# Gate/up pairs of a Strassen-Winograd feed-forward block: two kept products are added to each other by an accumulating SBUF transfer, and one low-part subtraction is issued later

## The reference, cut to what matters

```python
def swiglu(x, g, w_gu, w_down):
    gu = rmsnorm(x, g) @ w_gu
    return (jax.nn.silu(gu[..., :D_FF]) * gu[..., D_FF:]) @ w_down

# in trunk, for each layer i
x = x + swiglu(x, g_ffn[i], w_gu[i], w_down[i])
```

## Time and profile before

| | |
|---|---|
| median of three runs | 1248.07 us (1246.15 to 1248.12) |
| profiled execution, its own time | 1249.83 us |
| its span, first to last instruction | 1248.1 us |
| PE busy | 1216.1 us, 97% |
| DVE busy | 981.7 us, 79% |
| ACT busy | 655.7 us, 53% |
| POOL busy | 79.9 us, 6% |
| mean granted TensorE clock | 0.992 |

### The profile page before, as it was taken

How to read it: one execution, slowest core, us unless ns; L and a number is a source line. 1 busy time by engine, 2 the same in 40 slices (tenths; PEclk the granted TensorE clock), 3 DMA queues, 4 the chain that set the end, 5 groups by cost and what they waited for, 6 DMA issues and landing times. The chain is left out here.

```text
span 1248.1 us, 23025 instructions
## 1 busy us (share of the span) xinstructions
PE 1216.1 (97%) x8976; PEld 1170.6 (94%) x8976; DVE 981.7 (79%) x1600; ACT 655.7 (53%) x1178; POOL 79.9 (6%) x110
## 2 busy tenths in 40 slices
PE   6999999999999999999999999999999999999996
PEld 6997999999999999999989976799999999999996
DVE  4766558999999999975765476556999999999972
ACT  6656434454555555556754367533555555555542
POOL 1000000001001001102001100000001000100102
PEclk8998999999999999999999999999999999999998
DMA  7244122216425433525343210022225433532622
GB/s 223 81 132 128 35 85 85 68 51 147 111 71 125 116 94 94 139 85 155 133 129 122 88 65 2 1 85 85 68 60 132 119 90 95 126 102 82 157 64 85
DMA packets 196915, 122.13 MB, mean 98 GB/s; under 512 B 6091, under 2 KB 189035, under 8 KB 196808
## 3 DMA queue, kind: packets, MB, share of 16 engines
q1 hardware_dynamic: 185800, 101.24, 27.7%
q0 software_dynamic: 10816, 19.36, 6.8%
q10 hardware_dynamic: 192, 0.06, 0.0%
HBM read 106.67 MB, written 6.90 MB: 91 GB/s over the span
## 5 line engine op out<-in xcount | busy, mean ns | idle before, releaser
L1055 ACT ACTIVATE WH<-RAW 128x1024 fp32r<-128x1024 f32 (+2 forms) x149 | 144.2, 968 | 147.0 <-PE ACCP L1751 119.7
L1073 ACT ACTIVATE EH<-SB 128x1024 fp32r<-128x1024 f32 (+1 forms) x116 | 112.6, 971 | 166.7 <-DVE SB L1385 86.7
L1360 DVE TENSOR_TENSOR WL<-RAW,WH 128x1024 fp32r<-128x1024 f32 (+2 forms) x149 | 166.1, 1115 | 37.1 <-ACT WH L1055 35.9
L1391 DVE TENSOR_TENSOR EL<-SB,EH 128x1024 fp32r<-128x1024 f32 (+1 forms) x116 | 128.7, 1110 | 5.1 <-ACT EH L1073 2.8
L1751 PE MATMUL ACCP<-XH,WH 128*128 128x288 f32 x512 | 112.1, 301 | 3.7 <-DVE XL L1494 3.7
L1751 PE MATMUL ACCP<-XL,WH 128*128 128x288 f32 x512 | 110.3, 297 | 0.0
L1751 PE MATMUL ACCP<-XH,WL 128*128 128x288 f32 x512 | 110.3, 297 | 0.0
L1761 PE MATMUL MISC<-BH,EH 128*128 128x288 f32 x360 | 106.8, 297 | 1.6 <-DVE EL L1391 1.5
L1761 PE MATMUL ACCP<-BH,EH 128*128 128x288 f32 x360 | 106.8, 297 | 0.0
L1761 PE MATMUL MISC<-BL,EH 128*128 128x288 f32 x360 | 106.2, 295 | 0.0
L1761 PE MATMUL ACCP<-BL,EH 128*128 128x288 f32 x360 | 106.2, 295 | 0.0
(11 more groups left out here) (318 smaller groups left out, 3445.1 us busy)
## 6 DMA issues: line engine op xcount, KB each, us to landing
RAW<-in_w_gu SPq DMA_DIRECT2D x88, 512.0 KB, 3.9
RAW<-in_w_down SPq DMA_DIRECT2D x48, 384.0 KB, 4.2
RAW<-in_w_in SPq DMA_DIRECT2D x16, 512.0 KB, 4.4
RAW<-in_w_mem_kv SPq DMA_DIRECT2D x16, 512.0 KB, 3.6
RAW<-in_w_out SPq DMA_DIRECT2D x16, 512.0 KB, 4.1
X<-PC POOLq DMA_DIRECT2D x48, 144.0 KB, 2.9
RAW<-in_w_down SPq DMA_DIRECT2D x16, 256.0 KB, 2.9
RAW<-in_w_kv SPq DMA_DIRECT2D x8, 512.0 KB, 3.8
```

The source lines that it names most:

```text
L1055: a.activation(panel_in(WH, w % SPLIT_SLOTS, p), panel_in(RAW, p % RAW_SLOTS, p), ACT.Copy).then_inc(split_ready(w, True)[0], 1)
L1073: a.activation(EH[:, first:first + n, 0:nh], mixtures(s)[:, first:first + n, 0:nh], ACT.Copy).then_inc(block_hi, n)
L1360: v.tensor_tensor(panel_in(WL, w % SPLIT_SLOTS, p), panel_in(RAW, p % RAW_SLOTS, p), panel_in(WH, w % SPLIT_SLOTS, p), ALU.subtract).then_ ...
L1391: v.tensor_tensor(EL[:, first:first + n, 0:nh], mixtures(s)[:, first:first + n, 0:nh], EH[:, first:first + n, 0:nh], ALU.subtract).then_in ...
```

## The change

There are two parts.

1. In gate/up pairs `third_sum` is gone. Once all three copies are made, POOL issues a transfer that adds PC 1 to PC 2 in SBUF (semaphore `kept_summed`), and `second_sum` waits for that and adds U1 and the sum. The semaphore `up_right`, which `third_sum` raised, is replaced by `u_ready` where others waited for it.
2. `blocks_lo(k0)` is no longer issued after lead (3, 0), but in the first pair behind `hidden` of the last lead.

```diff
-                   (3, 0): [("lo", 6), ("blocks_lo", k0)], (3, 1): []}
+                   (3, 0): [("lo", 6)], (3, 1): []}
...
-            return (up_right, s.c + 1) if s.which == "gu" else (x22_done, 16 * (s.c + 1))
+            return (u_ready, 2 * s.i + 2) if s.which == "gu" else (x22_done, 16 * (s.c + 1))
...
+                elif s.kind == "pair" and s.which == "gu":
+                    gp.wait_ge(copied, 3 * s.i + 3)
+                    gp.dma_start(PC[:, s.i % 2, 2], PC[:, s.i % 2, 1], accum_op=ALU.add).then_inc(kept_summed, 16)
                 elif s.kind == "pair" and s.which == "down":
...
             def second_sum(s):
-                dve.wait_ge(copied, 3 * s.i + 3)
+                dve.wait_ge(kept_summed, 16 * (s.c + 1))
                 dve.wait_ge(u_ready, 2 * s.i + 1)
                 v.tensor_tensor(TU[:, HALF:T], U1[:], PC[:, s.i % 2, 2], ALU.add).then_inc(u_ready, 1)
-
-            def third_sum(s):
-
-                dve.wait_ge(u_ready, 2 * s.i + 2)
-                v.tensor_tensor(TU[:, HALF:T], TU[:, HALF:T], PC[:, s.i % 2, 1], ALU.add).then_inc(up_right, 1)
...
-                elif s.kind == "prepare_blocks_lo":
-                    blocks_lo(s.k)
...
                         take_lead(s.before)
                         split_lo(s.before.sn + 2)
                         hidden(s.before)
+                        blocks_lo(s.layer * HPAIRS * MIXED_PARTS)
...
                     if s.which == "gu":
                         second_sum(s)
-                        third_sum(s)
```

More of the change, by code:

```diff
@@ L726, in encoder_kernel @@
         block_done, copied = sem("block_done"), sem("copied")
-        u_ready, up_right, crossed = sem("u_ready"), sem("up_right"), sem("crossed")
+        u_ready, kept_summed, crossed = sem("u_ready"), sem("kept_summed"), sem("crossed")
         gate_right = sem("gate_right")
```

## The result

The changed kernel took 1254.2 us, median of 6 runs (1251.99 to 1257.67); the kernel before, on the same chip, 1248.28 us (6 runs, 1246.15 to 1249.89). The ratio is 1.0048, with a 95% interval of 1.0036 to 1.0059: slower by about 6 us, where 1247.2 us was forecast and the range ended at 1250.8. It is the sign of rival C, 2 us beyond that rival's own figure. The profiled execution took 1254.47 us, its span 1252.4 us.

The account below looks back on a forecast made before the run. PE, busy 97% of the span, was taken as the bound, with at most 7.6 us to gain from a faster DVE. Terms -0.3 - 1.2 + 0.6 = -0.9 us from 1248.07 gave 1247.2 us, range 1244.8 to 1250.8 us.

Parts of the forecast that it names:

- rival C: Last gate/up pair of each layer: its transfer is late and the kernel slower, +4.1 us, 1252.2 us; chance 0.11.
- Start of the layer, -0.3 us: Up to the first down pair: first EL wait shrinks, HBL wait grows; -0.13 us a layer, -0.3 us for both.
- small waits: PE at products 6 of pair 1 and 1 of pair 2: new waits, a few tenths each, none counting.
- Short waits, -1.2 us: Seven unlisted PE waits in gate/up pairs or the first down pair behind them: counted as gone, -1.2 us.
- DVE's relief: Whole kernel: DVE busy down by 16 us (36 x 0.46) with no gain in time to match.
- First gate/up pairs behind down pairs, nothing: Pair 17 and its like, six: sum there between 419.0 and 420.2, at most 0.2 us late; nothing lost.
- The last gate/up pair, +0.3 us a layer: Pairs 29 and 59: DVE waits for the transfer, PE loses 0.3 us a layer, +0.6 us; bounds 0 and 2.8.
- Pairs 28 and 58 ... nothing: 3.3 us between copy and second_sum, then 1 us in which DVE waits for PE: nothing lost.
- The end of the program: Around the span: 1.7 us taken over from the profiled execution before, with no term for the change.
- B: PE's waits in the pairs: DVE's relief reaches all of them, -7.6 us, 1240.5 us; chance 0.09 with half-way cases.
- D: Whole kernel: transfers slow weight loads as much as DVE gives, or short waits aren't DVE's; 1248.1 us, chance 0.10.
- The two rules of the Trainium skill: New transfer: some 2.3 us estimated, not used; GpSimd issue stalls during certain VectorE copies, two-input adds excepted.

Follow-up runs that it names:

- e1: Kernel before with all 36 third sums by transfer, low part of set k0 in its old place: 1249.74 us against 1248.04, ratio 1.0007.
- e2: Kernel before with only the low part of set k0 moved into the first pair, no transfers: 1251.43 us, ratio 1.0024.
- e7: Kernel before with transfers in the last three gate/up pairs of each layer alone (6 of 36), low part in its old place: 1251.54 us, ratio 1.0018.
- e8: Kernel before, no transfers, with ten extra second sums in the last gate/up pair of each layer: 1258.04 us, ratio 1.0074.
- e9: Kernel before with the transfer in the last gate/up pair of each layer alone (2 of 36): 1250.42 us, ratio 1.0006.
- e11: Kernel before with transfers only in the first gate/up pair behind each of the first two runs of down pairs (4 of 36): 1250.78 us, ratio 1.0010.
- e10: Kernel before, no transfers, with six extra second sums in the last gate/up pair of each layer: 1251.44 us, ratio 1.0026.
- e6: Changed kernel with the third w_down panel's load held until the layer's last transfer has landed: 1250.22 us, ratio 1.0010.
- first trace: Profiled execution of the changed kernel in its first measurement: 1254.47 us, span 1252.4 us.
- e3: Changed kernel with DVE's own third sum in the last gate/up pair of each layer, 34 transfers instead of 36: 1248.81 us, ratio 1.0003.
- e4: Kernel before with transfers only in chunks 4 to 6, 8 to 12 and 14 to 18 (26 of 36), low part in its old place: 1245.52 us, ratio 0.9971.
- Second trace: Profile from running the unmodified changed kernel once more: median 1253.53 us against 1249.29 for the kernel before, ratio 1.0034.

## Why the prediction was wrong, point by point

- *Start of the layer, -0.3 us*: -0.05 us a layer measured, -0.13 forecast. The chain was right in its steps: the first EL wait gone, the two "small waits" come (259 and 263 us). The HBL wait is as long as before, 1.0 us, and not the 2 us that stood among the signs: the small waits took the rest, for which the prediction had left room. The first down pair stands at 274.01 - 237.54 = 36.47 us from the start of the pairs against 36.02 before: +0.45 where +0.36 was worked out. e1 and e2 show the two halves, -1.48 and +1.43 us, against -1.47 and +1.34 in the terms: (3 x 0.49) and (2.16 less 0.82).
- *Short waits, -1.2 us*: not borne out, though the stretches look like it (-0.84 and -0.18 us over pairs 4 to 29 of the two layers). Most of it isn't the change's. The kernel before loses 0.76 us in pairs 9, 11 and 13 of layer 0 in its own trace; but e2, e7, e8, e9 and e11, in which DVE makes the third sum of those pairs itself, lose at most 0.09 us there, and only e10 has the loss again. In the traces of before and e10 ACT waited 2.0 us for a w_gu panel near 302 us, in the others at most 1.1 us; that this is the cause is argued, not shown. What the transfers do take away, in trace after trace, stands at the first down pair behind a row of gate/up pairs: 0.06 to 0.15 us each, some 0.2 us a layer, so 0.4 us in all. The term was read from one execution. The stretch of layer 0 varies by 2.0 us over the thirteen traces (259.8 to 261.8 us), with the transfer of pair 17 and with chance of this kind.
- *DVE's relief*: 16.8 us busy less, with no time gained to match. Right.
- *First gate/up pairs behind down pairs, nothing*: wrong in some executions. The sum was put at 419.0 to 420.2 us, from the typical and the slow row; it started at 420.29 in one trace (`cross` stood at 420.37 in the earlier trace rows: harmless), and 1.2 to 1.7 us later in three others, measured from the start of pair 4, where PE paid 1.4 to 1.9 us. The landing there was 6.0 to 7.5 us, more than the longest of the earlier trace rows.
- *The last gate/up pair, +0.3 us a layer*: this is the step that failed. The place and the queue behind it were right, and so, nearly, was the slack: 3.7 us by the prediction, 3.9 measured. The term, 0.6 us in all, was mis-sized three times over. First, it took a landing near the typical for a moment at which the DMA engines are always loaded. The trace of before had it, in a stretch cut to the transfer's own time, from the third copy's end on, and in the queue of SyncE:

```profile
537.60:540.90 3.30, 3.30 (x27) 3.30 (x27) 2.00 (x5) 0.41 (x1) 0.00 (x0) 1.00 0.76 224
```
```profile
536.08 1.47 SPq L915 DMA_DIRECT2D RAW<-in_w_down  x3
```

I had averaged over 7 us (0.38), and the half of it lies outside the burst. "Only the slowest of 48 landings is that slow" counted mostly quiet landings against a busy one; those of the last three pairs' transfers are 4.1 to 6.8 us. That it is the loads is shown by e6. By the slack of 3.9 us this alone cost 1.4 us in the first trace and 3.6 in the second. Second, it let the third copy end where it ended before. But ACT's copies stand behind FFNH, and DVE's earlier wait in pair 58 moved them 1.7 us. "Pairs 28 and 58 ... nothing" was true for PE directly (e3), and false for pair 59 behind; that is shown by e9 beside e7. It is so in layer 1 alone, and cost 1.7 us in the first trace and 1.0 in the second. Third, it priced PE's idle at its own length. Beyond it came some 1.5 us of half clock, in layer 1 of one trace of the change, and in both layers of e8. The term came to 0.48 + 4.05 = 4.5 us in one trace and 1.78 + 2.79 = 4.6 us in the other.
- *The end of the program*, put at nothing: the prediction took the 1.7 us around the span over from before, and no term for what 36 more transfers do there. Behind the last product stands a DRAIN of POOL, and the span ends 0.2 us behind it. Before, and with the change:

```profile
L536 POOLq DRAIN  x1: 4719/4719/4719, 1243.1 to 1243.1; - x1
```
```profile
L536 POOLq DRAIN  x1: 5495/5495/5495, 1246.7 to 1246.7; - x1
```

It rises with the number of new transfers, to within 0.1 us, whatever else the kernels do: 4.72 us with none (four traces) and with 4 (e11), 4.76 with 2, 4.80 with 6, 5.17 with 26, 5.41 with 34, and 5.50 us with 36 (four traces). Around the span the executions have 2.0 us with 36 transfers and 1.7 with none. Together that is 1.1 us of the loss. Why a DRAIN takes longer behind more transfers is open.
- *The rivals*: C had mechanism, place and sign. Its price of 2.8 us a layer came from one slow landing and left out the cascade and the clock; its chance of 0.11 was that of an accident, though the loads are there in every layer. By the rows above it deserved the larger chance. B is out: the HBL wait stands. Of D, the first half is out, as in the middle of the rows the transfers cost nothing (e4); its second half, that the short waits are not DVE's, was mostly true.
- *The two rules of the Trainium skill*: the estimate of 2.3 us by the Trainium skill, "DMA: Bandwidth & Descriptors", section "Anatomy of one DMA — SWDGE (gpsimd) path", stayed below even the quickest landing, 2.6 us, and would have pointed further away from the result. The exception for two-input adds in the Trainium skill, "SBUF — State Buffer", section "Who interferes with whom", holds here: 33 of the 36 issues of the new transfer took 0.85 to 0.94 us, in rows in which DVE is 97% busy. The other three, at pairs 17, 37 and 57, took 1.18 to 1.20 us beside the same kinds of DVE instruction; what made them longer is open.

Put together, the terms add up to what was measured. First trace: 4.5 us in the last chunks and 1.1 at the end, less 0.1 at the start of the layers and 1.0 in pairs 4 to 29, is 4.5 us; with 0.1 us by which its pairs start later, 4.6, and it took 4.64 us longer than the profiled execution of before (1254.47 against 1249.83). Second trace: 4.6 and 1.1 us, less 0.1, plus 0.7 in pairs 4 to 29 is 6.3 us; less 2.1 by which its pairs start earlier, 4.2, and it took 4.21 us longer. By the medians the two measurements gave 5.9 and 4.2 us.

## What to carry to other kernels

Where a wait for a transfer is added, take its price from the load of just that moment, over a stretch no longer than the transfer: a landing of 2.7 us in most pairs was 4 to 7 us where a burst of weight loads ran, and such bursts come at the same point each time. Then follow what the waiting engine feeds on the other engines, up to the issue of the next transfer of the same kind; a wait that costs nothing where it stands may take the slack from the next. Don't take a few tenths in one execution's trace for a standing cost: look whether a second trace has them. And split such an edit by place: in 26 pairs, with the low part in its old place, the transfer gained 2.5 us (e4); in all 36, likewise with the low part in its old place, nothing is left of that (e1, 1.7 us above the kernel before by the medians, 0.9 by the ratio).

## What the runs showed of the hardware

- An accumulating SBUF to SBUF transfer of 144 KB lands 2.6 to 3.1 us from its issue, mostly 2.7, in the middle of the rows of gate/up pairs, where the DMA share over its own time is 0.34 to 0.51, and 2.9 to 7.5 us where weight loads bring that share to 0.56 to 0.90, from the same queue and by the same instruction. The share alone doesn't tell which: pairs 7 and 47 have 2.9 to 3.5 us at 0.70 to 0.88.
- The DRAIN of POOL at the end of the program took 4.72 us behind 94 transfers issued by POOL in all, and 5.50 us behind 130; some 0.02 us for each transfer more.
- PE's granted clock went to about half (0.50 to 0.58) behind some idles and not behind others: in both layers of e8 (0.62 and 1.82 us), behind 1.82 us in the first trace of the changed kernel, but not behind 1.54 and 1.81 us in its second, nor behind 1.41 us in e1, 1.43 in e7 and 1.14 in e10. Each of the three times it cost 1.4 to 1.5 us. What tells the two traces of the same kernel apart stays open.
- The wake of POOL from ACT's last copy to the issue of the transfer took 0.3 us (1203.45 to 1203.74), half of the 0.60 taken from the down pairs. That made the transfers earlier than forecast, and was less than the landings were later.
